# Twelve of 32 experts run in pairs in six shared blocks, in an order that the chip works out

## What is computed

```python
grp = jnp.argmax(logits_c, axis=-1)                       # one of 4 groups
top_val, top_idx = lax.top_k(logits_f, 2)                 # two of its 8 experts
expert = grp[:, None] * EXPERTS_PER_GROUP + top_idx       # 32 experts, 2048 choices
...
def run_block(args):
    xe, e = args                                          # rows of expert e
    return (jax.nn.silu(xe @ w_gate[e]) * (xe @ w_up[e])) @ w_down[e]
...
y = y.at[slot_tok].add(yb * slot_gate[:, None])
```

## Time and profile before

| | us |
|---|---|
| median of 3 runs | 2381.63 (2381.39 to 2382.94) |
| span of the profiled execution | 2378.2 |
| first expert product starts | 610.14 |
| last expert block's end on TensorE | 1183.7 |
| one expert in the middle of the stage | 17.75 |
| TensorE busy in the span | 2244.8 |

### The profile page before, as it was taken

The page is one execution under the profiler, slowest core; times in us unless marked ns, Lnnn a source line. Parts: engine busy times, 40 slices in busy tenths (PEclk is TensorE's granted clock), DMA queues, the critical chain, the costliest instruction groups (busy, mean ns, idle before and its releaser), DMA issues.

```text
span 2378.2 us, 27108 instructions
## 1 busy us (share of the span) xinstructions
PE 2244.8 (94%) x10870; PEld 1688.5 (71%) x10870; DVE 1530.9 (64%) x1882; ACT 1177.5 (50%) x1669; POOL 379.4 (16%) x272
## 2 busy tenths in 40 slices
PE   7999998997899999999989999988999997999998
PEld 5877755674688888888768777744555476788876
DVE  5787287535799999999782265566655457423475
ACT  3265366501788888888753234354444513302321
POOL 2000022000211111111100000013555532000014
PEclk9999999998899999999989999999999998999999
DMA  3111010319999999999762101130010121211231
GB/s 125 55 52 36 1 72 1 128 56 416 342 375 379 387 385 397 395 394 380 275 214 68 48 18 28 40 109 0 1 36 18 59 92 71 65 53 38 95 125 54
DMA packets 107419, 349.85 MB, mean 147 GB/s; under 512 B 23644, under 2 KB 55205, under 8 KB 79256
## 3 DMA queue, kind: packets, MB, share of 16 engines
q1 hardware_dynamic: 94856, 322.72, 36.3%
q0 software_dynamic: 11232, 21.09, 2.4%
q10 hardware_dynamic: 1200, 4.24, 0.4%
HBM read 327.38 MB, written 37.40 MB: 153 GB/s over the span
## 4 chain that ended last, share of the span: by engine, by line
PE 83%; DVE 10%; ACT 4%; issue 2%; DMA 1%; SPq 0%; DVEq 0%; POOL 0%; ACTq 0%; POOLq 0%
PE psm L230 78%; DVE small L3218 2%; PE psm L1781 1%; ACT mem L1163 1%; PE psm L1085 1%; PE psm L470 1%; ACT mem L1121 1%; PE psm L1804 1%; DMA mem<-in_odd_w_out_dram 1%; DMA mem<-in_w_in_dram 1%; DVE mem L2923 0%; PE psm L1502 0%; DVE r L343 0%; DVE mem L1470 0%; DVE small L378 0%
## 5 line engine op out<-in xcount | busy, mean ns | idle before, releaser
L230 PE MATMUL psm<-r,r 128*128 128x512 f32 (+3 forms) x7294 | 1743.4, 396 | 42.7 <-issue 8.7
L230 PEld LDWEIGHTS psm<-r,r 128*128 128x128 f32 (+2 forms) x7294 | 1354.1, 189 | 397.7 <-issue 63.9
L343 DVE TENSOR_TENSOR r<-mem,r 128x1024 fp32r<-128x1024 f32 (+1 forms) x456 | 527.1, 1203 | 138.4 <-ACT r L334 133.0
L334 ACT ACTIVATE r<-mem 128x1024 fp32r<-128x1024 f32 (+1 forms) x456 | 442.7, 1037 | 53.5 <-DMA mem<-in_w_in_dram 22.3
L230 PE MATMUL psm<-mem 128*64 128x128 f32 (+12 forms) x2230 | 340.1, 422 | 17.2 <-DMA mem<-in_ada_w_dram 7.0
L230 PEld LDWEIGHTS psm<-mem 128*64 128x64 f32 (+6 forms) x2230 | 171.0, 161 | 143.1 <-issue 99.8
L3432 POOL TENSOR_TENSOR mem<-mem 128x1024 f32<-128x1024 f32 x63 | 152.6, 2422 | 161.6 <-ACT mem L3384 106.9
L3384 ACT ACTIVATE mem<-psm 128x512 f32<-128x512 f32 x160 | 94.4, 596 | 141.8 <-PE psm L230 135.0
L3218 DVE TENSOR_REDUCE small<-psm 128x1 f32<-128x1280 f32 x64 | 95.2, 1488 | 85.9 <-PE psm L230 85.9
L265 ACT ACTIVATE small<-small 128x1 f32<-128x1 f32 (+3 forms) x26 | 7.7, 295 | 225.8 <-DVE small L380 151.6
L3556 POOL TENSOR_TENSOR mem<-mem 128x1024 f32<-128x1024 f32 x14 | 33.6, 2402 | 400.9 <-ACT mem L3523 400.9
(11 more groups left out here) (342 smaller groups left out, 1754.0 us busy)
## 6 DMA issues: line engine op xcount, KB each, us to landing
mem<-in_exp_w_gate_dram SPq DMA_DIRECT2D x64, 1024.0 KB, 7.3
mem<-in_exp_w_up_dram SPq DMA_DIRECT2D x64, 1024.0 KB, 7.7
mem<-in_exp_w_down_dram SPq DMA_DIRECT2D x64, 1024.0 KB, 7.1
mem<-in_ada_w_dram SPq DMA_DIRECT2D x16, 1024.0 KB, 15.2
mem<-in_odd_w_in_dram SPq DMA_DIRECT2D x10, 1024.0 KB, 5.4
mem<-in_x_dram SPq DMA_DIRECT2D x16, 512.0 KB, 6.8
mem<-in_w_in_dram SPq DMA_DIRECT2D x8, 1024.0 KB, 5.4
mem<-in_ada_w_dram SPq DMA_DIRECT2D x16, 512.0 KB, 14.2
```

The lines of the kernel that those rows point to most:

```text
L230: return p.e.matmul(o, l, r, start=start, stop=stop, skip_group_check=True)
L334: p.e.activation(h, mem(self.raw(i), [R * n])[:, w * q:w * q + w], ACT.Copy).then_inc(*self.hi_done.up(i, q))
L343: p.e.tensor_tensor(l, mem(self.raw(i), [R * n])[:, w * q:w * q + w], h.bitcast(F32), SUB).then_inc(*self.lo_done.up(i, q))
```

## The change

Experts 0 and 1 stay first (`HEADS`). The chip ranks the other 30 by their count of rows, fullest first, with ties by number. Ranks 0 to 19 have a block each (`SINGLES`). Ranks 20 to 31, the twelve emptiest, share six blocks, two to a block with 64 slots each (`PAIRS`). So there are 26 blocks instead of 32, in the order 0 to 4, pair, 5 to 7, pair, 8 to 10, pair, 11 to 13, pair, 14 to 16, pair, 17, 18, pair, 19.

```diff
+HEADS = 2
+PAIRS = 6
+SINGLES = NEXP - 2 * PAIRS
+NMB = SINGLES + PAIRS
+NBLK = NMB + NOV
...
+        def rank_vector(p):
+            e = p.e
+            e.memset(KEY[:, 0:1], 2.0 ** 25)
+            e.memset(KEY[:, 1:2], 2.0 ** 24)
+            p.then(e.scalar_tensor_tensor(KEY[:, HEADS:32], CN[:, HEADS:32], 4096.0, cst("eidx")[:, HEADS:32], MUL, SUB), rt_dve, "key")
+            p.then(e.tensor_tensor(RIVAL, KEY.unsqueeze(1).broadcast_to([128, 32, 32]), KEY.unsqueeze(2).broadcast_to([128, 32, 32]),
+                                   ALU.is_gt), rt_dve, "rival")
+            p.then(e.tensor_reduce(RANK, RIVAL, AX, ADD), rt_dve, "rank")
+            p.then(e.tensor_scalar(SPARE, RANK, -float(SINGLES), 0.0, ADD, MAX), rt_dve, "paired")
+            p.then(e.tensor_scalar(CAPS, RANK, float(SINGLES), -64.0, ALU.is_ge, MUL), rt_dve, "caps")
+            p.then(e.tensor_copy(KEY, RANK), rt_dve, "place of expert")
+            p.then(e.scalar_tensor_tensor(RANK, SPARE, -0.5, RANK, MUL, ADD), rt_dve, "block of expert")
...
+        def order_vector(p):
...
+            p.then(e.tensor_tensor(RIVAL, KEY.unsqueeze(1).broadcast_to([128, 32, 32]),
+                                   cst("iota")[:, 0:32].unsqueeze(2).broadcast_to([128, 32, 32]), ALU.is_equal), rt_dve, "whose place")
+            p.then(e.tensor_tensor(RIVAL, RIVAL, cst("iota")[:, 0:32].unsqueeze(1).broadcast_to([128, 32, 32]), MUL), rt_dve, "expert there")
+            p.then(e.tensor_reduce(SPARE, RIVAL, AX, ADD), rt_dve, "order")
+            e.tensor_copy(ORDER, SPARE[:, HEADS:32]).then_inc(*rt_dve.up("experts in order"))
...
+                if rank not in whose:
+                    p.wait_ge(*rt_dve.at("experts in order"))
+                    whose[rank] = p.e.value_load(ORDER[0:1, rank - HEADS:rank - HEADS + 1], min_val=0, max_val=31)
...
+        def block_products(p, n, ps, x, xf, mine, c, s_, first, end):
+
+            if not whole_weights(n):
+                w = WE.two[mine[0]]
+                return mm3(p, ps[:, :], Two([x.hi], [x.lo]), Two([w.hi[c]], [w.lo[c]]), 0, slice(0, 128), s_, first, end)
+            for m, i in enumerate(mine):
+                r = slice(64 * m, 64 * m + 64)
+                _, _, R, w = pieces[i]
+                last = mm(p, ps[r, :], xf[:, r], mem(WE.raw(i), [R, w])[:, c, s_], first, end)
+            return last
...
         def experts_scalar(p):
-            for i in range(2):
+            for i in range(3):
                 WE.split_scalar(p, i)
+            p.wait_ge(*rt_dve.at("tab"))
+            turn_scalar(p, 0)
             ada_rows(p, 2)
-            WE.split_scalar(p, 2)
-            p.wait_ge(*rt_dve.at("tab"))
-            p.wait_ge(*ada_out.at(11))
-            turn_scalar(p, 0)
             product_scalar(p, 0, 0, None)
```

More of the change, by code:

```diff
@@ L305, in halves, with fetch @@
                 return h, rounded(kb + 8 + w / 256, w)
-            def fetch(self, p, i, *first):
+            def fetch(self, p, i, *first, found=None):
                 kb, srcs, R, n = self.pieces[i]
@@ L1480, in norm2_scalar @@
             rsqrt(p, rs8, sq8, 1, n2_act, "rs").then_inc(*n2_act.up("rs"))
+            p.e.activation(BELOW, cst("sltu"), ACT.Copy)
+            p.e.activation(EVERY, cst("ones"), ACT.Copy).then_inc(*n2_act.up("whole"))
             for q in range(2):
@@ L1753, in experts_pool @@
             mods_pool(p)
-            for e in range(2, NEXP):
+            for e in range(2, NMB):
                 p.wait_ge(*moe_dve.at("hd", e - 2))
@@ L1815, in down_tensor @@
                 for o in range(2):
                     for j in range(2):
-                        last = mm3(p, pss[o][:, :], x, WE.two[i], j, slice(0, 128), slice(512 * o, 512 * o + 512),
-                                   q + j == 0, q == 1 and j == 1)
+                        last = block_products(p, n, pss[o], Two(cols([h], 4)[2 * q + j], cols([l], 4)[2 * q + j]), HF[n % 2][:, 2 * q + j, :],
+                                              mine, j, slice(512 * o, 512 * o + 512), q + j == 0, q == 1 and j == 1)
@@ L1819, in down_tensor, with ahead @@
                     last.then_inc(*moe_pe.up("y", n, q, o))
-                WE.frees(i, moe_pe.at("y", n, q, 1))
-        def ahead_scalar(p, i):
-            if i + 3 < len(pieces):
-                WE.split_scalar(p, i + 3)
-        def ahead_vector(p, i):
-            if i + 3 < len(pieces):
-                WE.split_vector(p, i + 3)
+                for i in mine:
+                    WE.frees(i, moe_pe.at("y", n, q, 1))
+        def ahead(mine):
+            return [i + 3 for i in mine if i + 3 < len(pieces) and not whole_weights(source[i + 3][4])]
```

221 lines of the change are left out of this document (146 added, 75 removed).

## The result

| | before | after |
|---|---|---|
| median, us | 2381.56 (2381.39 to 2382.94) | 2365.44 (2364.99 to 2366.5) |
| span of the profiled execution | 2378.2 | 2364.7 |
| first expert product starts | 610.14 | 613.39 |
| last expert block's end on TensorE | 1183.7 | 1167.35 |
| experts' stage | 573.6 | 554.0 |

The medians differ by 16.1 us. The ratio is 0.9936, 95% interval [0.9924, 0.9948], which is 15.2 us of the kernel before, with an interval from 12.4 to 18.1. The forecast was 33.0 us faster. So the direction was right, and the gain is a little under half of what was said.

A forecast was written before the change was run, and what follows sets the result against it. The prediction took TensorE as the bound before the change and the transfers after it: 2381.6 - 32.3 (experts from the first pair on) - 0.7 (start) = 2348.6 us, range 2331 to 2376 us.

The forecast's parts named there:

- the likeliest case: Experts from the first pair on: transfers become the bound at about 410 GB/s, 2331 to 2369 us; chance 0.70.
- 184.5 MB at 410 GB/s: Experts from the first pair on: weights, rows and context of 27 experts take 450.0 us to move, against 479.3 today.
- The 3 us "taken": Experts from the first pair on: the 10.3 us that pieces lie ahead of use shrinks by 3, giving 447.0 us.
- The mechanism: Experts from the first pair on: transfers replace TensorE as the bound, bandwidth passes 400 GB/s, a gain of 32.3 us.
- a sign of being wrong: Pair blocks: the prediction is wrong if TensorE waits for VectorE's or ScalarE's splits behind them; no size given.
- The pair block: TensorE's work for two experts sharing a block: 20.9 us of products plus 1.2 of transposes, 22.1 us against 35.5 today.
- The slower rivals: Experts' stage: TensorE's clock falls (chance 0.06), halves run in turn (0.02), SP is late (0.03), a pair overflows (0.01).
- the halves run side by side: Pair blocks: two 64-column products take 0.87 us together; the rival, one after the other, gives 2431 us, chance 0.02.
- SP's reads: Experts' stage: reading 30 numbers for addresses set at nothing; the rival has up to 60 us, 2408.6 us, chance 0.03.
- no pair overflowed: Pair blocks: a rival had a pair exceed 64 slots, so the 15 spare blocks run; no price given, chance 0.01.
- clock rival: Pair blocks: TensorE's clock halves, so each takes 44 us, 8.3 more than two experts today; 2430.7 us, chance 0.06.
- The start: Ahead of the first expert product: it starts at 609.4 us instead of 610.14, a gain of 0.7 us.

The follow-up runs named there:

- one-product run: Changed kernel, but single blocks make only the first of three products and no low parts of their weights; 2355.42 us, ratio 0.9897.
- half-bytes run: Changed kernel, but the six pair blocks load half of their weight bytes and use what they loaded twice; 2333.61 us, ratio 0.981.

## Why the prediction came out with half the gain

The forecast for the profiled span was 2345.2 us, and it is 2364.7, 19.5 us more. Three pieces make this up: 4.0 us in the start, 12.7 in the stage, 2.8 behind it. The time lies inside the stated range of 2331 to 2376 us, and inside that of the likeliest case, whose lower bound was 395 GB/s; what missed is the middle, and with it the size of the gain.

**The failed step: 184.5 MB at 410 GB/s.** "I take 410 GB/s, near the rows with a deep queue" is the term that was mis-sized. At the measured 401 GB/s it is 460.1 us instead of 450.0. The 3 us "taken" from the time that pieces lie ahead didn't appear in the sum either. Together that is 13.1 us, and 12.7 us are to be explained. That they agree so well is partly luck, since the sum treats all of the section alike: in the last 17 us of the stage the loads have landed (a DMA share of 0.40 and less), and the last hidden values are 4.4 us late where they were 0.8 us late before. The windows that I leaned on, 423 GB/s over 20 us and 416 over 8, were real but short, and held hardly any row traffic. The one-product run shows that nothing done on TensorE or VectorE would have reached 410: with both out of the way the mix moves 403 GB/s. The run without gathers shows that row gathers lower the rate (403 to 413 GB/s). What else keeps it below the 424 of the best slices, and why the first 80 us of the one-product run went at 418 GB/s, stays open.

**The mechanism was right in the main.** The transfers became the bound, the bandwidth rose above 400 GB/s from the first pair on, TensorE got waits, SP's total wait fell from 485.8 to 438.4 us, and a single block still takes 17.75 us in the first five. Where TensorE waits was wrong: behind the pair blocks at splits, not inside them, and I had listed that as a sign of being wrong. The half-bytes run shows that two of the three waits are the transfers all the same, since those for L2021 and L348 (25.8 of 39.3 us) go with the bytes. For the third, put down to `issue`, it isn't shown.

**The pair block** takes 23.2 us, not 22.1. Since the transfers set the pace, I take it that this cost nothing; no run tests it. The granted clock was 1.00 in all six pair blocks; it fell after some of the waits behind them, which gives a mean of 0.98 over 300 us. The slower rivals didn't come: the halves run side by side (0.895 us for two), SP's reads cost nothing (the run without pairs keeps 17.75 us), no pair overflowed. In the clock rival's price the 8.3 us for a pair don't follow from its 44 and 35.5 us, which make 8.5; nothing hangs on it.

**The start** was forecast at 609.4 us, with at most 1.5 us more, and came at 613.39. VectorE's work was priced right. The gather was taken with its old 4.38 us; it took 8.76, because the later table put it behind four pieces in the queue. The forecast named what was late next (VectorE's splits) but not what stood ahead of the moved transfer. The place of `order_vector` costs 10.6 us by its own experiment (8.3 by the spans, of which 6.3 at the first product). My sum held the 4.0 us of work in it, but not the late gather.

**Where the other gain went.** TensorE lost 80 us of work, but each pair gives only about 3 us. The distance between the two bounds was 17.75 against 17.23 us per expert, and that distance, over 27 experts, is 14 of the 19.6 us that the stage gained. The other 5.6 us lie in the last blocks; what makes them up is open. Work removed from TensorE beyond that distance buys nothing in the cycles: leaving out two of three products in the singles left them as they were.

Of the 2.8 us behind the stage nothing was tried. The medians differ by 16.1 us and the spans by 13.5, since a profile is of one execution: the changed kernel's was the slowest of its four, 2366.5 us. Of that 1.8 us lay outside of the span. In later executions of the kernel before it was 2.2 us, so some 1.2 of the 3.4 us given ahead of the prediction are the difference between two executions.

The simplest of the best versions that compute the whole is the one with `order_vector` behind the table, 2353.5 us, ratio 0.989. Variants with more edits on top of it measure the same (0.9886 at the lowest) or slower.

## What to carry to other kernels

When two bounds lie close, the trace only brackets the second one: its longest window with the same mix of transfers (388 GB/s here) is held back by the first bound, and its best short window (423) has another mix. The answer, 401, lay between them. A version of the kernel with the first bound's work left out measures it in one run. When an instruction is moved later, look at what gets issued in the meantime on every queue: here 4 us more on VectorE ahead of a gather made the gather itself take 8.8 us instead of 4.4, because SP's loads got in ahead. And a wait that was removed on an engine behind the saturated transfers came back elsewhere: three reorderings of splits and rows moved the waits about, and none made the cycle shorter.

## What was unexpected of the hardware

- The first indirect gather landed in 4.0 to 4.9 us (once 6.2) when it was issued ahead of the 1 MB loads, and in 8.1 to 9.2 us right behind three or four of them.
- 16 DMA engines at a share of 1.00 moved 388 GB/s over 300 us before the change, 403 after it, and 413 over 400 us without gathers. So here the share didn't tell how near the limit the transfers were.
- Without the gathers the mean rose from 403 to 413 GB/s, although they are 4% of the bytes.
- Two fp32 products of 64 columns, one to each half of the partitions, took 0.895 us together in the pair blocks (0.87 in another stage), against 0.95 us for one of 128 columns.
